# Two row transfers and one weight piece requested ahead of six gathers, and two weight pieces behind the third gather instead of the sixth

## What is computed

```python
for l in range(DEPTH):
    ...                                    # mixer, residual, layer norm, modulation
    glog = (hf @ w_group + b_group).astype(F32)
    gsel = jnp.argmax(glog, -1)            # a group for each token
    top_p, top_i = lax.top_k(jax.nn.softmax(elog_sel, -1), TOP_K_IN_GROUP)
    ...
    a = jnp.einsum("nd,edf->nef", hf, w_gate)
    u = jnp.einsum("nd,edf->nef", hf, w_up)
    hid = jax.nn.silu(a) * u * comb[..., None].astype(h.dtype)
    return jnp.einsum("nef,efd->nd", hid, w_down).reshape(B, T, D)
    ...                                    # residual, layer norm
```

## Time and profile before

| | |
|---|---|
| median of 3 runs | 1167.3 us (1166.11 to 1167.33) |
| profiled execution, its own time | 1165.15 us |
| its span | 1163.4 us |
| TensorE matmul busy | 1077.5 us, 93% |
| TensorE weight load, VectorE, ScalarE, GpSimd busy | 42%, 47%, 30%, 8% |
| moved by DMA | 328.08 MB, mean 282 GB/s |
| SP's queue / GpSimd's / ScalarE's | 299.92 / 20.68 / 6.94 MB |
| chain that ended last, by engine | PE 65%, DMA 19%, DVE 8%, ACT 3%, issue 3% |
| of it DMA of `w_moe` / of the gathers | 16% / 1% |

### The profile page before, as it was taken

One profiled execution on the slowest core, in us unless ns is written; L12 is line 12 of the kernel. 1 busy time (PEld: TensorE's weight loads), 2 busy tenths in 40 slices (PEclk: granted clock), 3 DMA queues, 4 the chain that ended last, 5 costly groups with the idle time before them and its releaser, 6 DMA issues.

```text
span 1163.4 us, 14032 instructions
## 1 busy us (share of the span) xinstructions
PE 1077.5 (93%) x4666; PEld 485.1 (42%) x4696; DVE 547.9 (47%) x1244; ACT 350.0 (30%) x600; POOL 97.8 (8%) x169
## 2 busy tenths in 40 slices
PE   6999999999889999999969999999978999999995
PEld 3444534434533333333335645654642333333332
DVE  2373231327654655555664222313764455555645
ACT  1352321312442222222233434331353222222213
POOL 4000000003420000000031000000520000000000
PEclk9999999999899999999989999999879999999998
DMA  9994448493698999999842323212577999999963
GB/s 371 420 391 163 190 190 308 176 413 134 257 389 340 404 401 412 406 388 399 325 177 113 128 72 118 77 53 98 217 278 319 359 381 416 410 398 419 408 244 122
DMA packets 51305, 328.08 MB, mean 282 GB/s; under 512 B 6144, under 2 KB 8784, under 8 KB 14528
## 3 DMA queue, kind: packets, MB, share of 16 engines
q1 hardware_dynamic: 44672, 299.92, 64.7%
q0 software_dynamic: 4832, 20.68, 4.7%
q10 hardware_dynamic: 1760, 6.94, 1.5%
HBM read 320.64 MB, written 6.88 MB: 282 GB/s over the span
## 4 chain that ended last, share of the span: by engine, by line
PE 65%; DMA 19%; DVE 8%; ACT 3%; issue 3%; SPq 1%; DVEq 0%; POOL 0%; ACTq 0%; POOLq 0%
PE bank L758 33%; DMA ring<-in_w_moe 16%; PE bank L1219 15%; PE bank L1256 5%; PE bank L1236 4%; PE bank L784 2%; DMA ring<-in_w_out 1%; DVE zT L1895 1%; PE bank L1271 1%; DMA region<-h_store,toki 1%; PE bank L1196 1%; PE bank L1245 1%; DMA tiny<-in_tiny 1%; SPq L504 1%; DVE lstat L1898 1%
## 5 line engine op out<-in xcount | busy, mean ns | idle before, releaser
L1219 PE MATMUL bank<-ring,region 128*64 128x512 f32 x976 | 225.4, 596 | 13.9 <-DMA ring<-in_w_moe 10.8
L758 PE MATMUL bank<-ring,hT 128*128 128x512 f32 x336 | 148.1, 596 | 0.0
L1219 PEld LDWEIGHTS bank<-ring,region 128*64 128x64 f32 x976 | 72.8, 137 | 136.1 <-issue 134.7
L1256 PE MATMUL bank<-region 128*128 128x512 bf16 x510 | 115.0, 379 | 5.3 <-issue 4.5
L1236 PE MATMUL bank<-ring,region 128*64 128x512 f32 x512 | 116.5, 598 | 0.9 <-ACT region L1761 0.9
L1771 ACT ACTIVATE region<-region 128x512 bf16<-128x512 f32 x60 | 37.7, 630 | 200.4 <-DVE region L2351 200.4
L758 PEld LDWEIGHTS bank<-ring,hT 128*128 128x128 f32 x336 | 62.8, 190 | 77.9 <-issue 76.8
L758 PE MATMUL bank<-ring,region 128*128 128x512 f32 x192 | 85.4, 597 | 5.0 <-ACT region L1719 1.6
L1256 PEld LDWEIGHTS bank<-region 128*128 128x128 bf16 x540 | 50.4, 98 | 81.6 <-issue 22.7
L2351 DVE TENSOR_TENSOR region<-bank,region 128x512 f32<-128x512 f32 x60 | 41.3, 691 | 86.6 <-PE bank L1236 86.5
L758 PE MATMUL bank<-hT,ring 128*128 128x384 f32 x224 | 77.5, 499 | 1.2 <-DMA ring<-in_w_in 1.2
(11 more groups left out here) (344 smaller groups left out, 1285.6 us busy)
## 6 DMA issues: line engine op xcount, KB each, us to landing
ring<-in_w_moe SPq DMA_DIRECT2D x195, 1024.0 KB, 8.9
ring<-in_w_mod SPq DMA_DIRECT2D x42, 1024.0 KB, 11.2
ring<-in_w_in SPq DMA_DIRECT2D x21, 1024.0 KB, 8.0
region<-in_w_mod SPq DMA_DIRECT2D x5, 1024.0 KB, 13.7
ring<-in_w_out SPq DMA_DIRECT2D x4, 1024.0 KB, 7.5
ring<-in_w_out SPq DMA_DIRECT2D x8, 512.0 KB, 7.0
region<-gate_store POOLq DMA_DIRECT2D x4, 1024.0 KB, 7.7
region<-in_lnrows POOLq DMA_DIRECT2D x4, 1024.0 KB, 10.9
```

Of the source, the lines that this page charges most:

```text
L758: ins = pe.matmul(out, lhsT, rhs, start=start, stop=stop, skip_group_check=True)
L1219: ins = pe.matmul(bank[6][u * CAP:(u + 1) * CAP, :], xs[:, k, u * CAP:(u + 1) * CAP], places[u][:, at:at + 2 * DE], start=k == 0, stop=k = ...
L1256: ins = pe.matmul(bank[2 * t + y][:, :], onehot[:, t * P:(t + 1) * P], part[:, c], start=False, stop=False, skip_group_check=True)
```

## The change

Three edits, in both layers. GpSimd requests the rows of norm 2l+1 before the gathers, not after them. SyncE requests the third early piece (`st0`) at once behind the six pieces of pair 0, before it waits for anything of the gathers; since this is now earlier than the reads of the modulation weights, it waits for `ranks` in layer 0. And the other two early pieces wait for the third gathered block, not for the sixth.

```diff
@@ SyncE
                 up_weights(0)
                 down_weights(0)
 
+                sp.wait_ge(S["heads_done"], l + 1)
+                if l == 0:
+                    sp.wait_ge(S["ranks"], 1)
+                sp.wait_ge(landed[0][1], 16 * (g0 // G + 1))
+                sp.dma_start(early_up[2], A["w_moe"][(l * NE + G) * 3 + 1]).then_inc(landed[0][1], 16)
+
                 sp.wait_ge(S["x_new"], NT * (2 * l + 1))
                 for half in (S["ht_a"], S["ht_d"]):
                     sp.wait_ge(half, NT * (2 * l + 1))
-                sp.wait_ge(rows_at[SC - 1], 16 * (l + 1))
+                sp.wait_ge(rows_at[ROW_GROUPS[1][-1]], 16 * (l + 1))
                 for u in range(G):
                     sp.wait_ge(landed[u][0], 16 * (g0 // G + 1))
                     sp.dma_start(early_up[u], A["w_moe"][(l * NE + G + u) * 3]).then_inc(landed[u][0], 16)
-                sp.wait_ge(S["heads_done"], l + 1)
-                sp.wait_ge(landed[0][1], 16 * (g0 // G + 1))
-                sp.dma_start(early_up[2], A["w_moe"][(l * NE + G) * 3 + 1]).then_inc(landed[0][1], 16)
...
@@ GpSimd
                 bring_rows(2 * l)
                 affine(2 * l)
+                bring_rows(2 * l + 1)
                 gather_rows(l)
                 if l == 0:
-                    bring_rows(1)
                     store_gate(1, 1)
...
-                else:
-                    bring_rows(3)
```

## The result

Over 22 runs of each, the changed kernel takes 1175.59 us in the median (1167.15 to 1183.86), the kernel before 1166.14 us (1159.32 to 1174.85). The ratio is 1.0072, 95% interval 1.0054 to 1.0091: slower by 8.4 us (6.3 to 10.6). Forecast were 1171.1 us, +3.8, in a range of 1165.5 to 1174.5; the measured time lies above it. The direction was right, the size too small by more than half.

A forecast was written before the change was run, and what follows sets the result against it. The front was taken as bound by VectorE's routing up to the first gather, then by gather, TensorE and ScalarE. 1.7 + 1.7 + 0.4 = +3.8 us on 1167.3 gave 1171.1 us, range 1165.5 to 1174.5.

The forecast's parts named there:

- (a): Rival at the first gathers: stores of `h` stay hidden, the gather waits for `toki` alone; 1167 to 1168 us, chance 0.28 (including no effect).
- (b): Rival in the expert loop: it starts with a lead, TensorE's waits for weights shrink; 1163.7 us, chance 0.14.
- what the change brings: Rows and early pieces behind the gathers were already hidden, so bringing them sooner gains 0, between 0 and 10.7 us.
- (c): Rival at the last gathers: fourth and fifth block late by 2 us in both layers; 1174 us, chance 0.08.
- the two for the stores: Before each layer's first gather: `h` stores land late beside rows and third piece; +1.7 us each, bounds 0 to 3.9 and 3.0.
- The rate: From 299 in layer 0 and 841 in layer 1: 5.03 and 5.15 MB move at 426 GB/s, taking 11.8 and 12.1 us.
- The end: At the last store of `h`: 1.0 us from its last bytes to its landing, giving 311.8 in layer 0.
- The step to the gather: From the last store's landing to the first gather in layer 0: the same 0.83 us as behind `toki`.
- The bounds: Cost at the first gather: 0 to 3.9 us in layer 0, 0 to 3.0 in layer 1, from two 128 KB state stores.
- The two pieces: Two other early pieces beside the last three gathers delay layer 1's fifth block: +0.4 us, bounds 0 and 1.3.
- The clock: Pair 1, partly at 1.2 for 2.4 GHz: a shifted front wins or loses 1.6 us; taken 0, bounds -1.6 and +1.6.
- GpSimd's own time: Issuing two row requests falls into GpSimd's idle time before `toki`: cost 0.

The follow-up runs named there:

- e12: Changed kernel without its last edit: rows and third piece ahead of the gathers, the two other pieces behind the last gathered block; ratio 1.0078 to before, +9.1 us.
- e5: Changed kernel, with GpSimd's masks for the next mixer waiting in layer 0 for TensorE's fourth pair; ratio 1.0106 to the kernel before, +12.4 us.
- e14: Changed kernel, with GpSimd's masks for the next mixer ahead of its four `wgt` requests, no further wait; ratio 1.0073 to the kernel before, +8.5 us.
- e15: Changed kernel, with the rows requested by SyncE instead of GpSimd at the same point; ratio 1.0086 to the kernel before, +10.0 us.
- e3: Kernel before with only the last edit: the two other early pieces wait for the third gathered block, not the last; ratio 1.0019, +2.2 us.
- e10: Kernel before, with GpSimd's masks for the next mixer waiting in layer 0 for pair 0's transposed hidden block, behind the `wgt` requests; ratio 0.9995, -0.6 us.
- e13: Kernel before, with GpSimd's masks ahead of its four `wgt` requests and waiting for pair 0's transposed hidden block; ratio 1.0012, +1.4 us.
- e1: Kernel before with only the rows moved: GpSimd requests them ahead of its gathers in both layers; ratio 1.0056, +6.5 us.
- e6: Kernel before with only the rows moved, requested by GpSimd right behind ScalarE's request of the third store of `h`; ratio 1.0020, +2.3 us.
- e2: Kernel before with only the third early piece moved as in the change, rows and two other pieces left behind the gathers; ratio 1.0026, +3.0 us.
- e4: Changed kernel, but rows and third piece wait until the three stores of `h` have landed; ratio 1.0094 to the kernel before, +10.9 us.

## Why the prediction was wrong

**The mechanism was right.** The stores of `h` land behind `toki`, the first gather starts late, everything behind moves. Rival (a), stores hidden, is excluded by every trace with both rows ahead. So is (b): the loop's waits are 5.6 and 4.4 us for 6.0 and 4.7, and readers gained nothing, as the part on what the change brings had it. (c), the nearest in time with 1174, had the wrong place: the fifth gather of the changed kernel takes 5.6 and 6.3 us for 6.0 and 6.2 before, and e12 without the two pieces is as slow. Only the sixth is late, 9.1 and 9.7 us for 6.2, and pair 0 comes no later for it.

**The terms that failed are the two for the stores, +1.7 us in each layer.** Five traces have rows and third piece ahead of the stores (changed, e5, e12, e14, e15), four have nothing ahead (before, e3, e10, e13). Their means, third store's request to first gather: layer 0 10.1 for 5.6 us, +4.6; layer 1 8.7 for 6.2, +2.5. To pair 0: layer 0 24.2 for 19.2, +5.0; layer 1 22.4 for 19.6, +2.8. At the first gather the two layers together lose 7.1 us; forecast were 3.4. At pair 0 they lose 7.8. The single traces lie wide apart (21.4 to 28.8 us in layer 0, 20.2 to 26.6 in layer 1), the changed kernel's own trace has 3.5 us over before's at pair 0, and the totals of the five kernels are +8.4 to +12.4. So the fronts carry most of the loss; that they carry all of it is not shown.

Four things in the working bear on the size:

- *The rate.* I let 5 MB move at 426 GB/s, the rate of the earlier trace rows in 322 to 327. Ahead of the stores it was 325 for 6 us in e12. (426 - 325) x 6 us is 0.6 MB, 1.4 us at 426, an estimate from one trace.
- *The end.* I took 1.0 us from the last bytes to the landing, from a stretch in which stores had the engines alone. Behind rows and beside the weight piece the last 3 us ran at 53 or 55 GB/s (e12, changed): 2 us more. In e15 the last 2 us ran at 160.
- *The step to the gather.* I added 0.83 us from the landing, as it is behind `toki`; behind a store it is 0.3 us (319.92 to 320.20 in the changed kernel). That was 0.5 us too much.
- *The bounds.* My upper bounds, 3.9 and 3.0 us at the gather, came from two stores of 128 KB and were passed: 7.5 us in e14, 4.2 in e5. A store of a quarter of the bytes, with other transfers ahead of it, gave no bound here. And I set the lead of rows over stores from one trace, where it differs between executions by up to 6.4 us.

For layer 0, 1.7 + 1.4 + 2 - 0.5 makes 4.6 us, and 4.6 was measured as the mean; the two corrections were read off single traces afterwards, so this is an estimate, not a test. Counted from the end of `affine`, the sum had the last store landed after 14.5 and 14.3 us. It took 16.7 to 19.6 in layer 0 and 15.2 to 16.1 in layer 1: too short by 2.1 to 5.1 us, and by 0.9 to 1.8.

**What held or didn't matter.** The two pieces: +0.4 forecast, e3 and e12 leave 0 to a few us, not to be told apart. The clock: pair 1 of layer 0 lost 1.7 us and that of layer 1 won 1.6 in the profiled pair, the ends of the forecast's bounds, with sum zero. GpSimd's own time I had priced at 0; what I missed there is that its requests and masks behind the gathers can fall on VectorE's copies, up to 1.4 us.

**What stays open:** why rows move at 314 to 325 GB/s on fully busy engines in that place and at 423 elsewhere; what makes the long end; what moves the stores' requests against the rows' from one execution to the next; and how the queues are served in detail. From 312 to 317 in the changed kernel, 125 packets of the third piece and 201 of the stores move in the same microseconds. A record doesn't name its engine, so it isn't seen whether each engine kept the order of requests there.

## What to carry to other kernels

A transfer that nobody needs yet isn't free because the engines look idle: ask what is requested behind it, and whether that is on the path. Here 2 to 3 MB ahead of the stores cost 6.5 to 12.4 us (SyncE's rows alone 3.5), 3 MB behind the landed stores and ahead of the gathers 10.9, and 1 to 3 MB right behind the stores' requests 0.7 to 4.3. No kernel that moved these transfers was faster than the kernel before. Where such a move must be made, tie it to the request of the urgent transfer, not to its landing. Price a collision from the moment at which the bytes ahead are requested, with its slow end, and not by bytes over the best rate alone.

## What the runs showed of the hardware

- Transfers from different queues went in the order of their requests where the trace can tell: 175 packets of rows for one of a store that had been requested up to 4.8 us before (e1); 3.8 us for a store requested 0.67 us ahead of 2 MB (e6), 6.8 us for one requested 0.17 us behind 1 MB (e2). The order isn't strict: in e1's next 3 us, 181 packets of stores and 66 of rows moved together.
- With rows and third piece ahead, the third store landed 17.5 to 19.0 us (layer 0) and 14.6 to 15.2 (layer 1) after GpSimd's request of the rows, whether it was itself requested 4.6 or 12.2 us after it (changed, e5, e12, e14).
- The same 1 MB rows moved at 423 GB/s behind other transfers (e4) and at 325 and less ahead of the stores (e12), with the engines' share at 0.99 to 1.0 in both.
- Two copies of VectorE took 0.91 us alone, 1.13 beside a transfer request of GpSimd (e5), 1.33 beside a memset and two affine_selects (e13), and 1.94 beside a request, a memset and the start of an affine_select (changed).
